# Strassen block products in the down-projections of two squared-ReLU MLPs, with weight sums on GpSimd

## What is computed

```
def squared_relu_mlp(h, w_up, w_down):
    return jnp.square(jax.nn.relu(h @ w_up)) @ w_down

for layer in range(2):
    h = rms_norm(x, norm_mix[layer])
    y = conv_rwkv_mixer(h, ...) if layer == 0 else swa_sink_mixer(h, ...)
    x = x + y
    x = x + squared_relu_mlp(rms_norm(x, norm_mlp[layer]), mlp_up[layer], mlp_down[layer])
```

## Time and profile before

| | us |
|---|---|
| median of three runs | 2553.79 |
| lowest and highest run | 2542.37, 2571.63 |
| profiled execution | 2545.33 |
| its span, first to last instruction | 2543.5 |
| PE busy | 2424.6 (95%) |
| VectorE, ScalarE, GpSimd busy | 1059.4, 651.5, 219.2 |

### The profile page before, as it was taken

One profiled execution on the slowest core, in us unless ns is written; L12 is line 12 of the kernel. 1 busy time (PEld: TensorE's weight loads), 2 busy tenths in 40 slices (PEclk: granted clock), 3 DMA queues, 4 the chain that ended last, 5 costly groups with the idle time before them and its releaser, 6 DMA issues.

```text
span 2543.5 us, 38932 instructions
## 1 busy us (share of the span) xinstructions
PE 2424.6 (95%) x16722; PEld 1977.4 (78%) x16722; DVE 1059.4 (42%) x1286; ACT 651.5 (26%) x1002; POOL 219.2 (9%) x149
## 2 busy tenths in 40 slices
PE   6999979998999999999999999778999999999999
PEld 5888867787778888888888787446788888888887
DVE  3444477885333333333333432773333333233332
ACT  4011035444121211121122222562222112111212
POOL 0000021111330000000000400332300000000000
PEclk7999979999999999999999999999999999999999
DMA  3221100001111111111111121001111111111112
GB/s 111 66 82 47 49 2 4 3 3 44 42 42 42 58 41 49 49 49 49 49 49 42 38 56 33 1 1 33 33 58 42 50 50 49 49 49 41 58 41 83
DMA packets 166155, 110.83 MB, mean 44 GB/s; under 512 B 3599, under 2 KB 163685, under 8 KB 166053
## 3 DMA queue, kind: packets, MB, share of 16 engines
q1 hardware_dynamic: 163756, 100.39, 13.1%
q0 software_dynamic: 2240, 8.91, 1.1%
q10 hardware_dynamic: 56, 0.01, 0.0%
HBM read 102.49 MB, written 6.29 MB: 43 GB/s over the span
## 4 chain that ended last, share of the span: by engine, by line
PE 90%; DVE 7%; ACT 1%; issue 1%; DMA 0%; SPq 0%; POOL 0%; DVEq 0%; ACTq 0%
PE ps L263 70%; PE ps L333 7%; PE ps L701 2%; PE ps L723 1%; PE ps L1409 1%; DVE probs L1437 1%; PE ps L291 1%; DVE softmax_stats L1442 1%; PE ps L1223 1%; PE ps L1378 1%; DVE diag_x L1037 1%; DVE probs_t_b L1470 0%; PE ps L732 0%; PE ps L883 0%; DVE stage L1751 0%
## 5 line engine op out<-in xcount | busy, mean ns | idle before, releaser
L263 PE MATMUL ps<-h_hi,w_hi 128*128 128x512 f32 x1824 | 568.8, 393 | 23.9 <-DVE h_lo L414 10.2
L263 PE MATMUL ps<-h_lo,w_hi 128*128 128x512 f32 x1824 | 564.8, 391 | 0.0
L263 PE MATMUL ps<-h_hi,w_lo 128*128 128x512 f32 x1824 | 564.4, 391 | 0.0
L224 ACT CAST w_hi<-w_raw 128x1024 fp32r<-128x1024 f32 x180 | 189.3, 1052 | 949.1 <-PE ps L263 828.5
L263 PEld LDWEIGHTS ps<-h_hi,w_hi 128*128 128x128 f32 x1824 | 341.9, 189 | 97.6 <-issue 14.8
L263 PEld LDWEIGHTS ps<-h_lo,w_hi 128*128 128x128 f32 x1824 | 344.4, 189 | 72.5
L263 PEld LDWEIGHTS ps<-h_hi,w_lo 128*128 128x128 f32 x1824 | 344.2, 189 | 72.3
L501 DVE TENSOR_TENSOR residual<-residual,ps 128x1024 f32<-128x1024 f32 x128 | 156.2, 1220 | 340.5 <-PE ps L263 277.5
L228 DVE TENSOR_TENSOR w_lo<-w_raw,w_hi 128x1024 fp32r<-128x1024 f32 x180 | 219.6, 1220 | 100.9 <-ACT w_hi L224 100.9
L263 PE MATMUL ps<-mlp_hi,w_hi 128*128 128x512 f32 x768 | 237.0, 390 | 0.0
L263 PE MATMUL ps<-mlp_lo,w_hi 128*128 128x512 f32 x768 | 236.5, 389 | 0.0
(11 more groups left out here) (259 smaller groups left out, 2275.8 us busy)
## 6 DMA issues: line engine op xcount, KB each, us to landing
w_raw<-in_mlp_up SPq DMA_DIRECT2D x64, 512.0 KB, 3.9
w_raw<-in_mlp_down SPq DMA_DIRECT2D x64, 512.0 KB, 3.4
w_raw<-in_w_in_ab SPq DMA_DIRECT2D x26, 512.0 KB, 3.8
w_raw<-in_w_qkv SPq DMA_DIRECT2D x10, 512.0 KB, 3.8
x_in_tile<-in_x POOLq DMA_DIRECT2D x8, 512.0 KB, 4.3
w_raw<-in_w_out_ab SPq DMA_DIRECT2D x8, 512.0 KB, 3.6
w_raw<-in_w_o SPq DMA_DIRECT2D x8, 512.0 KB, 3.5
out<-out_chunk SPq DMA_DIRECT2D x8, 512.0 KB, 3.2
```

Of the source, the lines that this page charges most:

```text
L224: nc.scalar.copy(WH[:, slot], WR[:, slot]).then_inc(w_hi, 1)
L263: m = nc.tensor.matmul(acc(a_slot, half), ww, xx[:, k, half * HALF:(half + 1) * HALF], start=first, stop=last)
```

## The change

**Down-projection.** The eight output chunks of a group are taken as four pairs p = 0 to 3. For a pair, the weights (512 hidden x 256 outputs) and the squared activations (512 hidden x 1024 tokens) are each seen as 2x2 blocks: hidden chunks 0, 1 and 2, 3; outputs of the first and second chunk; tokens in halves. Instead of eight block products there are seven (p1 to p7), in Winograd's form of Strassen's algorithm, each of six matmuls of 512 columns. Three PSUM banks carry them for a pair: p1, then p6, p7 and p4 are accumulated in one (bank 4 or 5 by turns), p5 and then p3 in bank 7, p2 in bank 6. After each product VectorE adds the bank as it then stands to half a residual chunk; so the next product in that bank waits for that addition.

**Activation operands.** Up-products 0 to 2 go on as before, the fourth is made half by half (`up_by_halves`, tokens 512 to 1023 first). VectorE takes eight differences of halves (t1 to t4 for both chunks of a block), ScalarE makes their high parts and VectorE the low parts.

**Weight operands.** For each pair GpSimd makes four sums of 256 elements in a partition out of the raw weights, ScalarE copies them to their high part (1024 elements) and GpSimd makes their low part (1024 elements). VectorE makes the low part of the weights themselves only when the sums are done, since that frees the raw slot.

**Around it.** The SBUF of the pads of the attention's keys and values is in use by the new operands, so GpSimd clears them after `norm_pool` of the attention instead of before it. The distances for the attention are loaded after the last product of layer 0's MLP, behind the first two weight units of the next stage in SyncE's queue. ScalarE's first weight split of a group waits for the last product of the group before. `norm_pool` comes in GpSimd's queue behind the weight sums of all groups. Transposes of the output go to banks 0 to 3.

**The recurrence.** GpSimd's mask product waits for "tt" instead of "mtc".

```
-STAGE = {"in": (0, 0), "out": (26, 26), "mlp0": (34, 34), "qkv": (98, 130), "wo": (108, 140),
-         "mlp1": (116, 148)}
+STAGE = {"in": (0, 0), "out": (26, 26), "mlp0": (34, 34), "qkv": (98, 66), "wo": (108, 76),
+         "mlp1": (116, 84)}
...
+            def block_product(bank_n, wh, wl, bh, bl, new):
+                for c in range(2):
+                    for ww, xx in ((wh, bh), (wh, bl), (wl, bh)):
+                        m = nc.tensor.matmul(PS[:, bank_n, :], ww[:, c], xx[:, c], ...)
+                return m
...
+                dn_pe.done(block_product(x_bank, ah[:, 0:2, 0], al[:, 0:2, 0], B11H, B11L, True), f"p1_{p}")
+                t.wait_ge(s_lo, 4 * G + (p + 1))
+                if p:
+                    dn_dve.wait(t, G, f"p3_{p - 1}")
+                dn_pe.done(block_product(z_bank, sh[:, 0], sl[:, 0], M1H, M1L, True), f"p5_{p}")
+                if p:
+                    p4(p - 1)
+                dn_dve.wait(t, G, f"p1_{p}")
+                op_lo.wait(t, G, "t2_1")
+                dn_pe.done(block_product(x_bank, sh[:, 1], sl[:, 1], M2H, M2L, False), f"p6_{p}")
+                if after and p:
+                    after(t, 2 * p - 2)
+                if p < 3:
+                    p3()
+                    p2()
+                    if after and p:
+                        after(t, 2 * p - 1)
+                    p7()
+                else:
+                    p2()
+                    p7()
...
+                    p3()
+                    p4(3)
...
         def chunk_done(engine, name, k):
-            a_next = STAGE[name][1] if name in STAGE else A_END
-            engine.wait_ge(acc_free[k % 2], (a_next - 8 + k) // 2 + 2)
+            if name in ("qkv", "end"):
+                last = f"p4_{k // 2}" if k % 2 else "p3_3" if k == 6 else f"p2_{k // 2}"
+                dn_dve.wait(engine, NG - 1 if name == "qkv" else 2 * NG - 1, last)
...
+        def mlp_act(act, l, g, last=False):
...
+            sums_dve.wait(act, G, "t3_0")
+            hi(M3H[:, 0], M3R[:, 0], "t3_0")
+            sums_dve.wait(act, G, "t4_0")
+            hi(M4H[:, 0], M4R[:, 0], "t4_0")
+            sums_hi(1)
+            act.wait_ge(half_staged, G + 1)
+            square(B2R[:, 1, 1], "r3b")
...
+        def mlp_pool(pool, l, g):
+            for d in range(4):
+                w, raw = by_block(WR[:, d % 2]), WSR[:, d % 2]
+                a11, a12, a21, a22 = w[:, 0:2, 0], w[:, 2:4, 0], w[:, 0:2, 1], w[:, 2:4, 1]
+                pool.wait_ge(w_load[d % 2], 16 * (n + 2 + d // 2) + 16)
+                if d < 2:
+                    pool.wait_ge(acc_done, a0_ + 4 * g + 3)
+                else:
+                    dn_pe.wait(pool, G, f"p7_{d - 2}")
+                TT(raw[:, 0], a21, a22, ALU.add).then_inc(w_sum, 1)
...
+                TT(raw[:, 3], a12, raw[:, 1], ALU.subtract).then_inc(w_sum, 1)
+                pool.wait_ge(s_hi, 4 * G + (d + 1))
+                TT(WSL[:, d % 2], raw, WSH[:, d % 2].bitcast(F32), ALU.subtract).then_inc(s_lo, 1)
...
++            relu(B2R[:, :, 0], acc(0), ...).then_inc(acc_free[0], 1)
+            sums_done(dve, G, 0)
+            split_lo(dve, 0, u + 4)
+            squares.wait(dve, G, "r2")
+            combine(R[0][:, T1H], b22[0], R[0][:, T1H], "t2_0")
+            combine(m3[0], R[0][:, T1H], R[0][:, T0H], "t3_0")
+            combine(m4[0], b21[0], R[0][:, T1H], "t4_0")
+            lo(M2L[:, 0], R[0][:, T1H], M2H[:, 0], "t2_0")
+            lo(B2L[:, :, 0], B2R[:, :, 0], B2H[:, :, 0], "b2_0")
+            lo(M3L[:, 0], m3[0], M3H[:, 0], "t3_0")
+            lo(M4L[:, 0], m4[0], M4H[:, 0], "t4_0")
+            dve.wait_ge(half_done, G + 1)
+            relu(b22[1], acc(1, 1), RI[:, T1H]).then_inc(half_staged, 1)
+            squares.wait(dve, G, "r3b")
+            combine(R[1][:, T1H], b22[1], R[1][:, T1H], "t2_1")
+            combine(m3[1], R[1][:, T1H], R[1][:, T0H], "t3_1")
+            lo(M2L[:, 1], R[1][:, T1H], M2H[:, 1], "t2_1")
+            lo(B2L[:, 1, 1], b22[1], B2H[:, 1, 1], "b22_1")
+            lo(M3L[:, 1], m3[1], M3H[:, 1], "t3_1")
+            dve.wait_ge(acc_done, ag + 3 + 3)
+            relu(b21[1], acc(1, 0), RI[:, T0H]).then_inc(acc_free[1], 1)
+            squares.wait(dve, G, "r3a")
+            combine(m4[1], b21[1], R[1][:, T1H], "t4_1")
+            lo(B2L[:, 0, 1], b21[1], B2H[:, 0, 1], "b21_1")
+            products_1_5(0)
+            lo(M4L[:, 1], m4[1], M4H[:, 1], "t4_1")
+            product_6(0)
+            sums_done(dve, G, 1)
+            split_lo(dve, 1, u + 5)
...
@@ body_pool
-                lev_dve.wait(pool, n, "mtc")
+                lev_dve.wait(pool, n, "tt")
@@ block.sync
-            sp.wait_ge(w_lo, STAGE["mlp0"][0] + 1)
-            sp.dma_start(CON[:, C_DIST:], consts[:, C_DIST:]).then_inc(dist_in, 16)
             for j in two:
                 load_unit(sp, j, u0 + j, wqkv[:, :, S + P * j:S + P * j + P])
+            dn_pe.wait(sp, NG - 1, "p4_3")
+            sp.dma_start(CON[:, C_DIST:], consts[:, C_DIST:]).then_inc(dist_in, 16)
@@ block.gpsimd
             norm_pool(pool, "mlp0")
-
-            residual_done(pool, "mlp0")
+            with pool.Fori(0, NG) as g:
+                mlp_pool(pool, 0, g)
+            norm_pool(pool, "qkv")
+            residual_done(pool, "qkv")
             nc.gpsimd.memset(K2[:, :, :, :], 0.0).then_inc(pads_zero, 1)
...
-            norm_pool(pool, "qkv")
```

More of the change, by code:

```diff
@@ L313, in hybrid_trunk, with by_block @@
         acc_banks67 = PS[:, 6:8, :].rearrange("p b n -> p (b n)")
+        def by_block(ap):
+            return ap.rearrange("p (k m c) -> p k m c", k=4, m=2)
         def mlp_pe(t, l):
             u0, a0_ = STAGE[f"mlp{l}"]
[L318 to L333, removed]
-                                                 start=first, stop=last)
-                    if k == 3:
-                        i.then_inc(acc_done, 1)
@@ L338, in group, with up @@
-            def group(g, between, after=None):
[L339 to L347, removed]
+            def up(g, j, between=None):
+                product(t, j % 2, j % 2, a0_ // 2 + 2 * g + j // 2, u0 + 8 * g + j, 8, P, 0, Hh, Hl,
+                        ready=(h_lo, 8 * H_FILL[f"mlp{l}"]) if j == 0 else None, between=between)
@@ new lines, in up_by_halves @@
+            def up_by_halves(g):
+                t.wait_ge(w_lo, u0 + 8 * g + 3 + 3)
+                t.wait_ge(acc_free[1], a0_ // 2 + 2 * g + 1 + 1)
+                for half in (1, 0):
+                    for k in range(8):
+                        w_h, w_l = WH[:, 1, k * P:k * P + P], WL[:, 1, k * P:k * P + P]
+                        for ww, xx in ((w_h, Hh), (w_h, Hl), (w_l, Hh)):
+                            first, last = k == 0 and ww is w_h and xx is Hh, k == 7 and ww is w_l
+                            m = nc.tensor.matmul(acc(1, half), ww, xx[:, k, half * HALF:(half + 1) * HALF],
+                                                 start=first, stop=last)
+                    m.then_inc(half_done if half else acc_done, 1)
@@ L349, in mlp_pe @@
+            def group(g, between, after=None):
+                for j in range(3):
+                    up(g, j, between if j == 0 else None)
+                up_by_halves(g)
+                for p in range(4):
+                    down(g, p, after)
             group(0, norm_between(t, f"mlp{l}"))
@@ L485, in mlp_dve @@
         def mlp_dve(dve, l, g, last=False):
             u0, a0_ = STAGE[f"mlp{l}"]
[L487 to L502, removed]
+            ag, u, G = a0_ + 4 * g, u0 + 8 * g, 8 * l + g
@@ new lines, in mlp_dve, with relu, combine, lo @@
+            TT = nc.vector.tensor_tensor
+            def relu(dst, src, scale):
+                return nc.vector.scalar_tensor_tensor(dst, src, 0.0, scale, ALU.max, ALU.mult)
+            def combine(dst, a, b, step):
+                sums_dve.done(TT(dst, a, b, ALU.subtract), step)
+            def lo(dst, src, hi_, step):
+                op_hi.wait(dve, G, step)
+                op_lo.done(TT(dst, src, hi_.bitcast(F32), ALU.subtract), step)
+            def add(step, chunk, half, bank_n, before=None):
+                dn_pe.wait(dve, G, step)
+                if before:
+                    dn_dve.wait(dve, G, before)
+                xk = X[:, chunk, half * HALF:half * HALF + HALF]
+                dn_dve.done(TT(xk, xk, PS[:, bank_n, :], ALU.add), step)
@@ L615, in shift @@
                 .then_inc(shift_done, 1)
[L618 to L630, removed]
         two = (0, 1)
```

204 lines of the change are left out of this document (184 added, 20 removed).

## The result

The changed kernel took 2593.73 us in the median of four runs (2591.62 to 2597.39); the kernel before, with one more run beside it, 2549.57 (2542.37 to 2571.63). The ratio is **1.0165, with the interval 1.0128 to 1.0201**: slower, by more than the 1% that I had called the limit of "no change". The profiled execution has a span of 2590.7 us at a mean granted clock of 0.952, where before's had 2543.5 at 0.978.

What follows compares the result with a forecast made beforehand. PE, 90% of the chain, was taken as the bound. Matmuls -87.0, gaps +65.3, clock +32.0, attention's norm +14 and mask product -3 gave +21 us on 2545.3: 2566.6, stated as 2570, range 2498 to 2606.

Steps and rivals of the forecast that it cites:

- Matmuls removed: MLP down-products: 168 matmuls instead of 192 in each of 16 groups, saving 87.0 us and leaving 81.60 a group.
- Pairs 1 to 3: Later down-product pairs: PE's other products cover the waits for VectorE's additions, so 0 us lost.
- Pair 0: First down-product pair: PE's p6 waits for VectorE's late addition of p1, a gap of 1.69 us in every group.
- GpSimd's hold: Pair 0: GpSimd's low part of weight sums stops VectorE's two-input operations for 2.39 us, making the gap 4.08.
- The clock: Behind each group's gap: PE's granted clock at half pace for 4 us, costing 2.0 us a group.
- third rival: MLP groups: each gap brings 10 us at half clock, costing 5 instead of 2.0 us a group; 2614 us, 14%.
- A gap of 1.7 would lose nothing: MLP groups: a PE gap of 1.7 us would cost no clock.
- first rival: Pair 0: VectorE is not held by GpSimd, gap 1.69 us, clock full; -49 us, 2496 us, 22%.
- second rival: Pair 0: VectorE is held by GpSimd but the clock stays up; -11 us, 2535 us, 12%.
- The attention's norm: Norm after layer 0's MLP: GpSimd's squares come behind its weight sums, shifting all that follows by 14 us, once.
- The mask product: Recurrence: VectorE's 256-element steps no longer meet GpSimd's mask product, saving 3 us.
- The end, pads and distances: Output's last addition and transposes: 0, within 1 us; pad clearing and distance loading hidden by the attention norm's wait.

Runs made afterwards that it cites:

- b2: The changed kernel with ScalarE's copy of pair 1's weight sums later and VectorE's additions of p1 and p5 earlier; 2477.66 us, ratio 0.9700.
- a4: The changed kernel with 17 useless matmuls filling PE's gap in each MLP group; 2551.12 us, ratio 0.9971.
- c1: a4 with 12 useless matmuls instead of 17, leaving some 1.3 us of the gap open; 2551.25 us, ratio 0.9973.
- a3: The changed kernel with ScalarE's copy of pair 1's weight sums moved behind its second weight split; 2543.21 us, ratio 0.9937.
- b4: The changed kernel with only VectorE's additions of p1 and p5 in pair 0 moved earlier; 2541.67 us, ratio 0.9953.
- b1: The changed kernel with GpSimd's squares and additions at the attention's norm cut to 16 of 1024 tokens; 2582.88 us, ratio 1.0112.
- a2: The kernel before with only the mask product's wait changed to the later transpose; 2552.89 us, ratio 0.9964.
- a1: The changed kernel with GpSimd's mask product waiting for the copy of the block again, as before; 2607.05 us, ratio 1.0165.
- c3: b3 run again in more rounds; 2479.92 us, ratio 0.9676.
- b3: b2 with VectorE's low parts at the attention's norm ahead of its wait for GpSimd's sums, PE's norm matmuls a unit later; 2472.27 us, ratio 0.9674.
- c4: b3 with GpSimd's mask product waiting for the copy of the block again; 2483.51 us, ratio 0.9694.

## Why the prediction was wrong: slower, not unchanged

The prediction took "no change" as likeliest (0.44), at +21 us; it was +36 between the means of all runs, and +44 between the medians of the first ones, where the few runs of before lay low. The time stayed inside the range.

- **Matmuls removed, 87.0.** Right. b2 has groups of 81.65 us against the 81.60 that I took, so the products in one bank cost at most 0.05 us a group.
- **Throughput.** Right: sums of 0.74 us (0.72 assumed), no engine full. (From the rows, 1024 elements more cost GpSimd 2.23 us and not the 2.19 that I wrote; nothing hangs on it.)
- **Pairs 1 to 3.** Right: L383 waits 16 times, once a group, always for p1's addition in pair 0.
- **Pair 0, 1.69 us.** 1.86 with the hold gone: right to 0.2 us.
- **GpSimd's hold, 2.39 us.** 2.2. The gap is 4.04 where I said 4.08.
- **The clock, 2.0 us a group. This is the step that failed**, by its size: I took "4 us at half pace", from the stretch behind the third norm, and got 7.0 us at half clock. That is 2.7 us of time (a4 against after), and 0.3 us more stand beside the recorded wait in a4 and c1 too, at full clock, which my sum had not: 81.60 + 4.04 + 0.31 + 2.72 = 88.67 against 87.7. Over the sixteen groups the matmuls behind the gaps take 41.6 us longer than in a4 (2.6 on average), where I had 32.0 for the clock; that is 9.6, and the 0.3 make 5.0. With 0.6 less for the gaps it is **14 us**, nearly the whole distance between +21 and +36. My third rival had drawn the line for "over 1% slower" at 2.3 us of clock a group; it was crossed without the 10 us at half clock that the rival needed. The stretches that I had borrowed from the earlier trace rows were one each behind a norm, and they already ran from 0 to 10 us. That spread belonged to the likeliest case, not to a rival.
- **"A gap of 1.7 would lose nothing"** is wrong as well. In a3 and b4 1.86 us of gap brought 3.3 us at half clock and 1.6 us of time in 14 and 13 of 16 groups, though 2.65 us at the first norm had brought none. So the first rival was priced too low: a3 is what it described, and its mean is 15 us below before's, not 49. The second rival (held, clock up) is a4: 5 us below before instead of 11, which the 0.3 us a group explain.
- **The attention's norm, +14 us.** The addition came at E + 18.2 where I said E + 18, and the trace gives +14.5. The medians of b1 give 10.9; at full clock, by the slope above, it is 14.0.
- **The mask product, -3 us.** a2 against before is -3.0 us at full clock, after against a1 -3.5, c3 and b3 against c4 -1.5. Right, as far as a scatter of 2.2 us lets one tell.
- **The end, pads and distances.** No wait for them in the trace. Eight groups at +1.63 would make the last stage 13.0 us longer; it is 10.4 longer. Of the 2.6 between them 1.7 are the milder clock loss of the first groups of layer 1 (37.23 and 37.91 us behind the gap instead of 38.4); 0.9 are left, within the 1 us that I gave for the end.

## What to carry to other kernels

A wait of PE between dense matmuls has two prices, the wait itself and the clock behind it; here the second was two thirds of the first, and a gap half as long kept more than half of it (1.6 of 2.7 us). So, where a change that saves matmuls opens a gap in every iteration, take the gap to zero before judging the change: find which in-order step stands between the last operand and the release, and move that step ahead of waits that it doesn't need. A GpSimd operation beside two-SBUF-input work of VectorE belongs where VectorE is idle, not in the latency chain; where the gap can't be closed, matmuls without a use can fill it, as they did here.

## What the runs showed of the hardware that I had not expected

- Seventeen useless matmuls in each gap, or twelve, made the kernel 42 us faster: the granted clock stayed at 1.00 through both MLPs.
- The clock fell behind gaps of 4.04 us in every MLP group (7.0 us at half), and behind gaps of 1.86 us in most (3.3 us at half); it did not behind 1.3 us (c1), nor behind 2.65 us at a norm. Within a3 and b4 five gaps of the same 1.9 us cost nothing, so the length of the gap alone does not decide. What does stays open.
- Stretches of some 24 to 27 us at half clock come in the recurrence in other places in each execution (579 to 606 us in after's profile, 364 to 391 in a1's, 360 to 384 in a3's, 473 to 497 in a4's), with no gap that I could name ahead of them. Time at half clock is nearly all by which the runs of one kernel differ: 97 to 180 us before, times 0.41, is 34 us, and the 59 runs span 35.5. That it is these stretches that vary can be seen only in the profiled executions.
- The hold works in both directions: GpSimd's additions took 3.24 to 3.26 us instead of 2.34 beside VectorE's low parts, and its low part of the sums 2.90 instead of 2.37.
